# Expert gate/up product: all eight chunks as three fp32r passes, weights split in two halves

## The chip, the cores and the metric

The kernel runs on one core of a Trainium2 chip. The metric is the device time of one execution in microseconds (us). Engines are named as in the profile: PE (TensorE matmuls), PEld (TensorE weight loads), DVE (VectorE), ACT (ScalarE), POOL (GpSimd), SP (SyncE). An engine's name with a q (ACTq) is its instruction queue: register, semaphore and DMA-issuing instructions.

## The reference, cut to what matters

An encoder layer (attention, then a hierarchical mixture of experts) over 3072 tokens. The change touches only the experts. Tokens are sorted by expert into blocks of 128 rows, and each block runs one expert's gated MLP:

```python
D_MODEL, D_EXPERT, N_EXPERTS, MOE_BLOCK = 1024, 256, 32, 128

def run_block(args):
    tok, e = args
    xe = x[tok]                                           # 128 x 1024
    hid = jax.nn.silu(xe @ w_gate[e]) * (xe @ w_up[e])    # 128 x 256
    return hid @ w_down[e]                                # 128 x 1024
```

All of it is float32. A float32 product is made on PE in one of two ways: as one float32 matmul, or split, where each operand is a rounded part (hi, type fp32r) and the rest (lo, fp32r), and three fp32r matmuls hi·hi, hi·lo and lo·hi are summed in PSUM.

## The kernel before

The stages follow one another: projections, attention, output mix, routing, experts (`stage_experts`, from 3508 to 4208 us of the span), combine. In the expert stage there are 64 live blocks here. `over_blocks` runs them in pairs: blocks 0 and 1 written out, then a loop over pairs, whose number is read from a register. Each engine has its own hand-ordered body per block b, and s is b's parity. Nothing but semaphores ties the engines together, so the order within an engine's body is the order in which its work runs.

What one block needs: `x[s]` (gathered by POOL), its transpose in PSUM (`psX`, eight 128x128 transposes, `x_turn`), the gate/up product in `psG` (128 x 512: 256 gate and 256 up columns, over KC = 8 chunks of 128), SiLU (`act_g`) and product (`hid`), the transpose of `hid` (`psH`, `hid_turn`), the down product in `psY` (`down`, always three fp32r passes, 12 matmuls of 128x512), and the copy and store of `y` (`y_out`).

The gate/up product before: chunks 4 to 7 as float32 matmuls straight from `xT` and the loaded weights `w_gu` (L1908), chunks 0 to 3 (HK = 4) as 12 fp32r matmuls (L1913) from `xT_hi`, `xT_lo`, `wg_hi`, `wg_lo`.

The bodies before, for block b:

- PE (`body`): float32 chunks of b, fp32r chunks of b, `hid_turn(b-1)`, `x_turn(b+1)`, `down(b-1)`.
- ACT: `wg_hi` of b (L1792), `xT_hi` of b (L1796), `y_out(b-2)` with its DMA issue (L1811, L1813), `wd_hi` of b (L1806), `hT_hi` of b-1 (L1800), SiLU of b (L1825).
- DVE: copy `xT` (L1837), `xT_lo` (L1839), `wg_lo` (L1845), `wd_lo` (L1857), `hT_lo` of b-1 (L1850), `hid` of b (L1867).
- SP: the expert's weights (3 DMAs of 1 MB) where a block starts a new expert, into a ring of four experts (WS = 4).
- POOL: the gather of `x` one block ahead, released by `x_turn`.

`wg_round`, `wd_round`, `wg_rest` and `wd_rest` begin with `value_load`: the engine's queue reads the ring slot of the block's expert from the SBUF tile `eb` (L1790, L1804, L1843, L1854). `wg_hi` and `wg_lo` have one buffer, `wd_hi` and `wd_lo` two. In the kernel before nothing waits for the release of `wg_hi` by name: `wg_hi` of b stands behind SiLU of b-1 on ACT, which waits for all gate/up matmuls of b-1.

Of the kernel before, what the change touches and what calls it, by code (L numbers as in the profile page):

```python
# [13 lines left out]
P = 128  # L14
# [1652 lines left out]
def stage_experts(nc, t, eb, idx):  # L1667
# [3 lines left out]
    with ExitStack() as ctx:  # L1671
        def sb(name, shape, dt=F32):
            return ctx.enter_context(nc.sbuf_tensor("e_" + name, shape, dt))
# [32 lines left out]
        xT_psum, xT_ready = sem("xT_psum"), sem("xT_ready")  # L1706
# [77 lines left out]
        def _(act):  # L1784
# [3 lines left out]
            def wg_round(b):  # L1788

                w = act.value_load(eb[0:1, bass.ds(b + SLOT_AT, 1)], min_val=0, max_val=WS - 1)  # L1790
                act.wait_ge(w_ready, b + 1)
                nc.scalar.activation(wg_hi[:, :, :], w_gu[:, bass.ds(w * KC, HK), :], ACT.Copy).then_inc(wg_rounded, 1)  # L1792

            def xT_round(b):
                act.wait_ge(xT_psum, b + 3)
                nc.scalar.activation(xT_hi[:, :, :], psX[:, 0, :].rearrange("p (c n) -> p c n", n=P), ACT.Copy).then_inc(xT_rounded, 1)  # L1796

            def hT_round(b):
                act.wait_ge(hT_psum, b + 1)
# [34 lines left out]
        def _(dve):  # L1834
            def xT_out(b):
                dve.wait_ge(xT_psum, b + 3)
                nc.vector.tensor_copy(xT[:, :, :], psX[:, 1, :].rearrange("p (c n) -> p c n", n=P)).then_inc(xT_ready, 1)  # L1837
                dve.wait_ge(xT_rounded, b + 1)
                nc.vector.tensor_tensor(xT_lo[:, :, :], psX[:, 0, :].rearrange("p (c n) -> p c n", n=P),  # L1839
                                        xT_hi[:, :, :].bitcast(F32), ALU.subtract).then_inc(xT_rest_ready, 1)  # L1840

            def wg_rest(b):
                w = dve.value_load(eb[0:1, bass.ds(b + SLOT_AT, 1)], min_val=0, max_val=WS - 1)  # L1843
                dve.wait_ge(wg_rounded, b + 1)
                nc.vector.tensor_tensor(wg_lo[:, :, :], w_gu[:, bass.ds(w * KC, HK), :], wg_hi[:, :, :].bitcast(F32),  # L1845
                                        ALU.subtract).then_inc(wg_ready, 1)
# [13 lines left out]
            def body(b, j, s):  # L1860
# [6 lines left out]
                nc.vector.tensor_tensor(hid[:, s, :], act_g[:, :], psG[:, s, DE:2 * DE], ALU.mult).then_inc(hid_ready, 1)  # L1867

            pairs = over_blocks(dve, body)
            hT_out(2 * pairs - 1)  # L1870

        @block.tensor
        def _(pe):
            def x_turn(b, n, s):
                pe.wait_ge(x_loaded[s], 16 * n + 16)
                pe.wait_ge(xT_ready, b + 1)
# [25 lines left out]
            def body(b, j, s):  # L1902

                w = pe.value_load(eb[0:1, bass.ds(b + SLOT_AT, 1)], min_val=0, max_val=WS - 1)
                pe.wait_ge(w_ready, b + 1)
                pe.wait_ge(xT_ready, b + 2)
                for c in range(HK, KC):
                    nc.tensor.matmul(psG[:, s, :], xT[:, c - HK, :], w_gu[:, bass.ds(w * KC + c, 1), :].rearrange("p o n -> p (o n)"), start=c == HK, stop=False)  # L1908
                pe.wait_ge(xT_rest_ready, b + 1)
                pe.wait_ge(wg_ready, b + 1)  # L1910
                for c in range(HK):
                    for a, ww in ((xT_hi, wg_hi), (xT_hi, wg_lo), (xT_lo, wg_hi)):
                        i = nc.tensor.matmul(psG[:, s, :], a[:, c, :], ww[:, c, :], start=False,  # L1913
                                             stop=c == HK - 1 and ww is wg_hi and a is xT_lo)
                i.then_inc(g_psum, 1)
# [8 lines left out]
            pe.sem_inc(xT_ready, 1)  # L1924
# [222 lines left out]
```

## Time and profile before

| what | value |
|---|---|
| time, median of 3 runs (lowest to highest) | 4388.55 us (4384.7 to 4389.39) |
| span of the profiled execution | 4395.6 us |
| mean granted PE clock | 0.933 |
| PE busy | 3869.2 us (88%) |
| DVE busy | 2832.1 us (64%) |
| ACT busy | 2320.4 us (53%) |
| POOL busy | 415.9 us (9%) |

The span runs from the first to the last instruction of one profiled execution. A row of the timeline reads: start in us from the span's start, duration in us, engine, line, operation, output<-inputs, count, and in brackets the idle time just before it with what ended it; "<-issue" means that the engine's own queue was late. Matmuls are pipelined, so the recorded length of one (0.39 us) is longer than the distance from one start to the next (0.23 us). The granted clock is a share of full speed (2.4 GHz); 0.5 is the other level, 1.2 GHz.

### The profile page before, as it was taken

How to read it: one execution, taken by the hardware profiler on the slowest of the kernel's cores; microseconds unless marked ns; L12 is line 12 of the kernel's file. 1: busy time of each engine (PE TensorE's matmuls, PEld its weight loads, DVE VectorE, ACT ScalarE, POOL GpSimd, SP SyncE). 2: the span in 40 equal slices, each digit the busy share in tenths (PEclk: the TensorE clock that was granted, in tenths of full speed). 3: DMA queues.
4: the chain of work that ended last, by engine and by line, in shares of the span. 5: the costliest groups of instructions: out<-in, count | busy, mean ns of one | idle time of the engine just before them, and what ended most of it. 6: DMA issues, size and time to landing. Idle time of an engine off the chain costs nothing. (4 is left out here: it accounts for less than half of the span.)

```text
span 4395.6 us, 58559 instructions
## 1 busy us (share of the span) xinstructions
PE 3869.2 (88%) x16145; PEld 2606.2 (59%) x16146; DVE 2832.1 (64%) x4533; ACT 2320.4 (53%) x3960; POOL 415.9 (9%) x446
## 2 busy tenths in 40 slices
PE   7999985699999999999999999996999599999920
PEld 3444442366666666666676667664777466666710
DVE  3445454588887888887778677854444556666645
ACT  2222220277777777777666666676333055555521
POOL 0000000011111111111111111100000011111123
PEclk9999996699999999999999999998999699999965
DMA  2343337421122222212211221102333176776658
GB/s 99 105 140 120 125 110 192 155 59 41 24 57 58 59 58 49 46 27 58 57 40 24 57 58 40 24 7 98 134 129 123 39 256 243 254 260 244 240 207 280
DMA packets 295763, 482.81 MB, mean 110 GB/s; under 512 B 117136, under 2 KB 203664, under 8 KB 284750
## 3 DMA queue, kind: packets, MB, share of 16 engines
q1 hardware_dynamic: 207374, 347.24, 26.8%
q10 hardware_dynamic: 71888, 73.54, 4.8%
q0 software_dynamic: 16272, 59.25, 4.0%
q8 instruction: 109, 1.79, 0.2%
q14 instruction: 120, 0.98, 0.1%
HBM read 318.20 MB, written 161.78 MB: 109 GB/s over the span
## 5 line engine op out<-in xcount | busy, mean ns | idle before, releaser
L832 ACT ACTIVATE b_p_hi<-b_psS 128x512 fp32r<-128x512 f32 (+1 forms) x1376 | 821.1, 597 | 620.7 <-PE b_psS L963 579.9
L963 PE MATMUL b_psS<-b_q,b_k 96*128 96x512 f32 (+3 forms) x3440 | 1054.3, 404 | 55.1 <-ACT b_prob L835 31.9
L880 DVE TENSOR_TENSOR b_p_lo<-b_prob,b_p_hi 128x512 fp32r<-128x512 f32 x1152 | 829.0, 721 | 291.0 <-ACT b_prob L835 250.5
L835 ACT ACTIVATE b_prob<-b_psS 128x512 f32<-128x512 f32 (+1 forms) x1376 | 815.3, 593 | 1.1
L963 PEld LDWEIGHTS b_psS<-b_q,b_k 96*128 96x128 f32 (+3 forms) x3440 | 630.1, 186 | 286.5 <-ACT b_prob L835 39.5
L888 DVE TENSOR_REDUCE b_mx_s<-b_psM 128x1 f32<-128x512 f32 x1024 | 691.1, 687 | 80.9 <-PE b_psM L994 67.3
L994 PE MATMUL b_psM<-b_k,b_q 128*128 128x512 f32 (+1 forms) x1280 | 515.3, 424 | 58.1 <-DMA b_v<-V 45.9
L986 PE MATMUL b_psO<-b_p_hi,b_v_hi 128*65 128x512 f32 x1280 | 516.7, 404 | 26.1 <-DVE b_p_lo L880 24.3
L986 PE MATMUL b_psO<-b_p_hi,b_v_lo 128*65 128x512 f32 x1280 | 509.7, 398 | 0.0
L986 PE MATMUL b_psO<-b_p_lo,b_v_hi 128*65 128x512 f32 x1280 | 509.5, 398 | 0.0
L510 PE MATMUL a_psZ<-a_w_in,a_xT 128*128 128x512 f32 (+1 forms) x1200 | 405.9, 498 | 20.0 <-DMA a_w_in<-w_in 10.6
L994 PEld LDWEIGHTS b_psM<-b_k,b_q 128*128 128x128 f32 (+1 forms) x1280 | 251.7, 197 | 161.4 <-DVE b_mx_s L888 49.2
L510 PEld LDWEIGHTS a_psZ<-a_w_in,a_xT 128*128 128x128 f32 x1200 | 207.6, 190 | 219.3 <-issue 195.1
L821 POOL TENSOR_TENSOR b_p_lo<-b_prob,b_p_hi 128x512 fp32r<-128x512 f32 x128 | 167.5, 1309 | 1718.4 <-ACT b_prob L835 1718.4
L986 PEld LDWEIGHTS b_psO<-b_p_lo,b_v_hi 128*65 128x65 f32 x1280 | 175.8, 137 | 125.3 <-issue 5.5
L986 PEld LDWEIGHTS b_psO<-b_p_hi,b_v_hi 128*65 128x65 f32 x1280 | 176.8, 138 | 119.6 <-DVE b_p_lo L880 53.8
L986 PEld LDWEIGHTS b_psO<-b_p_hi,b_v_lo 128*65 128x65 f32 x1280 | 177.6, 139 | 110.5 <-issue 4.2
L1908 PE MATMUL e_psG<-e_w_gu,e_xT 128*128 x512 | 233.2, 598 | 9.4 <-SPq L1755 8.4
L1857 DVE TENSOR_TENSOR e_wd_lo<-e_w_dn,e_wd_hi 128x2048 fp32r<-128x2048 f32 x64 | 146.7, 2293 | 102.9 <-ACT e_wd_hi L1806 102.9
L888 DVE TENSOR_REDUCE b_mx_p<-b_psM 128x1 f32<-128x512 f32 x256 | 173.9, 687 | 30.8 <-PE b_psM L994 27.7
L287 ACT ACTIVATE a_z<-a_psZ,a_rstd 128x1184 f32<-128x1184 f32 x25 | 31.2, 1248 | 292.5 <-PE a_psZ L510 292.5
L1792 ACT ACTIVATE e_wg_hi<-e_w_gu 128x2048 fp32r x64 | 122.9, 1920 | 97.4 <-SPq L1755 75.1
(242 smaller groups left out, 4808.5 us busy)
## 6 DMA issues: line engine op xcount, KB each, us to landing
e_w_gu<-w_gate SPq DMA_DIRECT2D x32, 1024.0 KB
e_w_gu<-w_up SPq DMA_DIRECT2D x32, 1024.0 KB
e_w_dn<-w_down SPq DMA_DIRECT2D x32, 1024.0 KB
Y<-e_y ACTq DMA_DIRECT2D x64, 512.0 KB, 5.3
Y<-b_zeros ACTq DMA_DIRECT2D x4, 4096.0 KB, 27.2
a_x<-xall SPq DMA_DIRECT2D x25, 512.0 KB, 3.8
c_o<-O SPq DMA_DIRECT2D x24, 512.0 KB, 5.0
c_x<-xall SPq DMA_DIRECT2D x24, 512.0 KB, 3.6
```

Of the source, the lines that this page charges most:

```text
L510: i = nc.tensor.matmul(psZ[:, lo:hi], xT[:, c, :], w_in[:, c, lo:hi], start=c == 0, stop=c == KC - 1)
L821: nc.gpsimd.tensor_tensor(p_lo[:, slot, :], prob[0:kn, slot, :], p_hi[0:kn, slot, :].bitcast(F32), ALU.subtract).then_inc(lo_ready_pool, 1)
L832: nc.scalar.activation(p_hi[0:kn, (s * NI + j) % NP, :], psS[0:kn, j % 2, :], ACT.Exp)
L835: nc.scalar.activation(prob[0:kn, (s * NI + j) % NP, :], psS[0:kn, j % 2, :], ACT.Exp).then_inc(p_ready, 1)
L880: nc.vector.tensor_tensor(out, prob[0:kn, slot, :], p_hi[0:kn, slot, :].bitcast(F32), ALU.subtract).then_inc(lo_ready, 1)
L888: nc.vector.tensor_reduce(dst, psM[:, u % 2, :], AX.X, ALU.max).then_inc(m_free, 1)
L963: m = nc.tensor.matmul(psS[0:kn, j % 2, :], kk[s][0:r, k], qq[s][0:r, q], start=n == 0, stop=n == len(passes) - 1)
L986: m = nc.tensor.matmul(psO[0:VC, b % 2, :], vv[s][:, vc, :], pp[:, slot, :], start=first and n == 0, stop=last and n == 2)
L994: nc.tensor.matmul(psM[:, u % 2, :], q0[s][0:r, q * P:q * P + P], k0[s][0:r, kc:kc + 512], start=True, stop=True).then_inc(m_psum, 1)
L1792: nc.scalar.activation(wg_hi[:, :, :], w_gu[:, bass.ds(w * KC, HK), :], ACT.Copy).then_inc(wg_rounded, 1)
L1857: nc.vector.tensor_tensor(wd_lo[:, c, :], w_dn[:, bass.ds(w * HC, HC), :], wd_hi[:, c, :].bitcast(F32), ALU.subtract).then_inc(wd_ready, 1)
L1908: nc.tensor.matmul(psG[:, s, :], xT[:, c - HK, :], w_gu[:, bass.ds(w * KC + c, 1), :].rearrange("p o n -> p (o n)"), start=c == HK, stop=F ...
```

## The change

All eight chunks of gate/up are made as three fp32r passes. `xT` and its copy are gone, `xT_hi` and `xT_lo` have all eight chunks, `wg_hi` and `wg_lo` too, but they are filled in two halves of four chunks, each half in one buffer. ACT rounds a half (`wg_round(b, half)`), DVE makes its rest (`wg_rest(b, half)`), and PE runs 12 matmuls per half. A new semaphore `half_done` tells that the first half's matmuls of a block are done; ACT waits for it before it writes the first half of the next block. The small operations are reordered: `hT_hi`/`hT_lo` of b-2, SiLU and `hid` of b-1, and `wd_hi`/`wd_lo` of b-1 stand now in the body of b, and `y_out(b-2)` is the last of ACT's body. The diff, cut to its core:

```diff
-        xT = sb("xT", [P, KC - HK, P])
-        xT_hi, xT_lo = sb("xT_hi", [P, HK, P], F32R), sb("xT_lo", [P, HK, P], F32R)
-        wg_hi, wg_lo = sb("wg_hi", [P, HK, 2 * DE], F32R), sb("wg_lo", [P, HK, 2 * DE], F32R)
+        xT_hi, xT_lo = sb("xT_hi", [P, KC, P], F32R), sb("xT_lo", [P, KC, P], F32R)
+        wg_hi, wg_lo = sb("wg_hi", [P, KC, 2 * DE], F32R), sb("wg_lo", [P, KC, 2 * DE], F32R)
...
-            def wg_round(b):
+            def wg_round(b, half):
 
                 w = act.value_load(eb[0:1, bass.ds(b + SLOT_AT, 1)], min_val=0, max_val=WS - 1)
                 act.wait_ge(w_ready, b + 1)
-                nc.scalar.activation(wg_hi[:, :, :], w_gu[:, bass.ds(w * KC, HK), :], ACT.Copy).then_inc(wg_rounded, 1)
+                nc.scalar.activation(wg_hi[:, half * HK:half * HK + HK, :], w_gu[:, bass.ds(w * KC + half * HK, HK), :],
+                                     ACT.Copy).then_inc(wg_rounded, 1)
...
             def body(b, j, s):
-                wg_round(b)
+                if at_least(b, 1):
+                    act.wait_ge(half_done, b)
+                wg_round(b, 0)
+                if at_least(b, 2):
+                    hT_round(b - 2)
+                if at_least(b, 1):
+                    silu(b - 1, 1 - s)
                 xT_round(b)
-                if not isinstance(b, int) or b > 1:
-                    y_out(b - 2, j - 1, s)
-                wd_round(b, s)
-                if not isinstance(b, int) or b > 0:
-                    hT_round(b - 1)
-                act.wait_ge(g_psum, b + 1)
-                act.wait_ge(hid_ready, b + 1)
-                nc.scalar.activation(act_g[:, :], psG[:, s, 0:DE], ACT.Silu).then_inc(silu_ready, 1)
+                wg_round(b, 1)
+                if at_least(b, 1):
+                    wd_round(b - 1, 1 - s)
+                if at_least(b, 2):
+                    y_out(b - 2, j - 1, s)
...
+            # DVE
             def body(b, j, s):
-                xT_out(b)
-                wg_rest(b)
-                wd_rest(b, s)
-                if not isinstance(b, int) or b > 0:
-                    hT_out(b - 1)
-                dve.wait_ge(silu_ready, b + 1)
-                nc.vector.tensor_tensor(hid[:, s, :], act_g[:, :], psG[:, s, DE:2 * DE], ALU.mult).then_inc(hid_ready, 1)
+                wg_rest(b, 0)
+                if at_least(b, 2):
+                    hT_out(b - 2)
+                if at_least(b, 1):
+                    hid_out(b - 1, 1 - s)
+                xT_out(b)
+                wg_rest(b, 1)
+                if at_least(b, 1):
+                    wd_rest(b - 1, 1 - s)
...
+            # PE
             def body(b, j, s):
 
-                w = pe.value_load(eb[0:1, bass.ds(b + SLOT_AT, 1)], min_val=0, max_val=WS - 1)
-                pe.wait_ge(w_ready, b + 1)
-                pe.wait_ge(xT_ready, b + 2)
-                for c in range(HK, KC):
-                    nc.tensor.matmul(psG[:, s, :], xT[:, c - HK, :], w_gu[:, bass.ds(w * KC + c, 1), :].rearrange("p o n -> p (o n)"), start=c == HK, stop=False)
-                pe.wait_ge(xT_rest_ready, b + 1)
-                pe.wait_ge(wg_ready, b + 1)
-                for c in range(HK):
-                    for a, ww in ((xT_hi, wg_hi), (xT_hi, wg_lo), (xT_lo, wg_hi)):
-                        i = nc.tensor.matmul(...)
-                i.then_inc(g_psum, 1)
+                pe.wait_ge(xT_rest_ready, b + 2)
+                for half in range(2):
+                    pe.wait_ge(wg_ready, 2 * b + half + 1)
+                    for c in range(half * HK, half * HK + HK):
+                        for a, ww in ((xT_hi, wg_hi), (xT_hi, wg_lo), (xT_lo, wg_hi)):
+                            i = nc.tensor.matmul(psG[:, s, :], a[:, c, :], ww[:, c, :], ...)
+                    i.then_inc(g_psum if half else half_done, 1)
```

The rest of PE's body (`hid_turn(b-1)`, `x_turn(b+1)`, `down(b-1)`) is as before. After the last pair, ACT runs `hT_hi` of the last block but one, SiLU and `wd_hi` of the last block, `y_out`, `hT_hi` of the last block, `y_out`; DVE's end answers to it.

## Rows read from the trace of the kernel before

**Rows 1.** Windows: us, busy us (count) of PE, PEld, DVE, ACT, POOL, clock, DMA.
```profile
3600.00:3700.00 100.00, 99.24 (x405) 69.33 (x404) 64.62 (x56) 56.97 (x58) 10.24 (x18) 1.00 0.70 246
3800.00:3900.00 100.00, 99.15 (x410) 70.25 (x409) 63.89 (x59) 57.77 (x58) 11.26 (x20) 1.00 0.72 256
```

**Rows 2.** Groups by line and form, 3540 to 4190 us: busy us, mean ns | idle before.
```profile
L1908 PE MATMUL e_psG<-e_w_gu,e_xT 128*128 x496 | 222.9, 592 | 0.6 <-SPq L1755 0.6
L1845 DVE TENSOR_TENSOR e_wg_lo<-e_w_gu,e_wg_hi 128x2048 fp32r<-128x2048 f32 x63 | 144.4, 2293 | 11.4 <-issue 11.4
L1792 ACT ACTIVATE e_wg_hi<-e_w_gu 128x2048 fp32r x62 | 119.1, 1921 | 28.2 <-issue 21.9 <-SPq L1755 6.2
...
L1811 ACT ACTIVATE e_y<-e_psY 128x1024 f32<-128x1024 f32 x62 | 63.5, 1023 | 34.4 <-PE e_psY L1897 34.4
...
L1839 DVE TENSOR_TENSOR e_xT_lo<-e_psX,e_xT_hi 128x512 fp32r<-128x512 f32 x62 | 42.9, 692 | 103.2 <-ACT e_xT_hi L1796 103.2
...
L1850 DVE TENSOR_TENSOR e_hT_lo<-e_psH,e_hT_hi 128x256 fp32r<-128x256 f32 x62 | 26.3, 425 | 14.7 <-ACT e_hT_hi L1800 11.3
```

**Rows 3.** Timeline, one block's turn from its gate/up product to the next.
```profile
3859.41 3.59 PE L1908 MATMUL e_psG<-e_w_gu,e_xT 128*128 x8
...
3863.07 0.40 PE L1913 MATMUL e_psG<-e_wg_lo,e_xT_hi 128*128 128x512 f32 x1
...
3865.35 0.40 PE L1913 MATMUL e_psG<-e_wg_hi,e_xT_lo 128*128 128x512 f32 x1
...
3865.82 1.06 PE L1879 MATMUL e_psX<-e_ident,e_x 128*128 128x128 f32 x8
3866.02 0.38 ACT L1800 ACTIVATE e_hT_hi<-e_psH 128x256 fp32r<-128x256 f32 x1 [2.15 <-PE e_psH L1886]
...
3866.44 0.42 DVE L1850 TENSOR_TENSOR e_hT_lo<-e_psH,e_hT_hi 128x256 fp32r<-128x256 f32 x1
3866.78 0.41 DVE L1867 TENSOR_TENSOR e_hid<-e_act_g,e_psG 128x256 f32<-128x256 f32 x1
...
3866.96 0.47 PE L1897 MATMUL e_psY<-e_wd_hi,e_hT_hi 128*128 128x512 f32 x1
...
3869.80 2.74 PE L1908 MATMUL e_psG<-e_w_gu,e_xT 128*128 x6
```

**Rows 4.** Timeline, ACT and DVE around a store and a weight split.
```profile
3860.91 0.37 ACTq L1813 DMA_DIRECT2D Y<-e_y  x1
...
3861.95 1.92 ACT L1806 ACTIVATE e_wd_hi<-e_w_dn 128x2048 fp32r x1 [1.22 <-issue]
...
3864.02 2.29 DVE L1857 TENSOR_TENSOR e_wd_lo<-e_w_dn,e_wd_hi 128x2048 fp32r<-128x2048 f32 x1 [1.55 <-ACT e_wd_hi L1806]
```

**Rows 5.** Line 1790, the slot's read on ACT's queue: ns min/median/max.
```profile
L1790 ACTq TENSOR_LOAD <-eb x64: 274/280/288, 3509.1 to 4182.5; - x64
```

**Rows 6.** Timeline, the starts of blocks 2 and 63 on PE.
```profile
3547.60 3.59 PE L1908 MATMUL e_psG<-e_w_gu,e_xT 128*128 x8
...
4186.14 3.59 PE L1908 MATMUL e_psG<-e_w_gu,e_xT 128*128 x8
```

**Rows 7.** Timeline, the start of the stage: blocks 0 and 1.
```profile
3524.81 1.91 ACT L1792 ACTIVATE e_wg_hi<-e_w_gu 128x2048 fp32r x1 [68.90 <-SPq L1755]
3524.86 6.58 PE L1908 MATMUL e_psG<-e_w_gu,e_xT 128*128 x8 [7.78 <-SPq L1755]
...
3534.23 0.38 ACT L1825 ACTIVATE e_act_g<-e_psG 128x256 f32<-128x256 f32 x1 [3.92 <-PE e_psG L1913]
...
3540.53 0.47 PE L1913 MATMUL e_psG<-e_wg_hi,e_xT_hi 128*128 128x512 f32 x1 [0.75 <-DVE e_wg_lo L1845]
3540.84 0.39 PE L1913 MATMUL e_psG<-e_wg_lo,e_xT_hi 128*128 128x512 f32 x1
```

**Rows 8.** Timeline, the longest stall of PE in the stage and what follows.
```profile
4021.59 0.47 PE L1913 MATMUL e_psG<-e_wg_hi,e_xT_hi 128*128 128x512 f32 x1 [1.92 <-DVE e_wg_lo L1845]
...
4022.49 0.63 PE L1913 MATMUL e_psG<-e_wg_hi,e_xT_hi 128*128 128x512 f32 x1
4022.91 0.63 PE L1913 MATMUL e_psG<-e_wg_lo,e_xT_hi 128*128 128x512 f32 x1
```

**Rows 9.** Windows of 5 us around that stall, columns as in Rows 1.
```profile
4020.00:4025.00 5.00, 3.41 (x9) 2.72 (x10) 3.74 (x2) 1.92 (x1) 0.00 (x0) 0.72 0.83 284
```

More of the change, by code:

```diff
@@ L1705, in stage_experts @@
         cur_ready = sem("cur_ready")
-        xT_psum, xT_ready = sem("xT_psum"), sem("xT_ready")
+        xT_psum, half_done = sem("xT_psum"), sem("half_done")
         g_psum, silu_ready, hid_ready = sem("g_psum"), sem("silu_ready"), sem("hid_ready")
@@ L1734, in is_last, with at_least @@
             return isinstance(b, int) and b == BLOCKS - 1
+        def at_least(b, n):
+            return not isinstance(b, int) or b >= n
         @block.sync
@@ L1806, in wd_round, with silu @@
                 nc.scalar.activation(wd_hi[:, s * HC:(s + 1) * HC, :], w_dn[:, bass.ds(w * HC, HC), :], ACT.Copy).then_inc(wd_rounded, 1)
+            def silu(b, s):
+                act.wait_ge(g_psum, b + 1)
+                act.wait_ge(hid_ready, b + 1)
+                nc.scalar.activation(act_g[:, :], psG[:, s, 0:DE], ACT.Silu).then_inc(silu_ready, 1)
             def y_out(b, j, s):
@@ L1858, in wd_rest, with hid_out, body @@
                                         ALU.subtract).then_inc(wd_ready, 1)
[L1860 to L1865 removed]
+            def hid_out(b, s):
                 dve.wait_ge(silu_ready, b + 1)
                 nc.vector.tensor_tensor(hid[:, s, :], act_g[:, :], psG[:, s, DE:2 * DE], ALU.mult).then_inc(hid_ready, 1)
+            def body(b, j, s):
+                wg_rest(b, 0)
[7 more added lines that the diff above has]
+                    wd_rest(b - 1, 1 - s)
             pairs = over_blocks(dve, body)
+            hT_out(2 * pairs - 2)
+            hid_out(2 * pairs - 1, 1)
+            wd_rest(2 * pairs - 1, 1)
             hT_out(2 * pairs - 1)
@@ L1902, in body @@
             def body(b, j, s):
-                w = pe.value_load(eb[0:1, bass.ds(b + SLOT_AT, 1)], min_val=0, max_val=WS - 1)
-                pe.wait_ge(w_ready, b + 1)
-                pe.wait_ge(xT_ready, b + 2)
-                for c in range(HK, KC):
-                    nc.tensor.matmul(psG[:, s, :], xT[:, c - HK, :], w_gu[:, bass.ds(w * KC + c, 1), :].rearrange("p o n -> p (o n)"), start=c == HK, stop=False)
-                pe.wait_ge(xT_rest_ready, b + 1)
-                pe.wait_ge(wg_ready, b + 1)
-                for c in range(HK):
-                    for a, ww in ((xT_hi, wg_hi), (xT_hi, wg_lo), (xT_lo, wg_hi)):
-                        i = nc.tensor.matmul(psG[:, s, :], a[:, c, :], ww[:, c, :], start=False,
-                                             stop=c == HK - 1 and ww is wg_hi and a is xT_lo)
-                i.then_inc(g_psum, 1)
+                pe.wait_ge(xT_rest_ready, b + 2)
[3 more added lines that the diff above has]
+                        for a, ww in ((xT_hi, wg_hi), (xT_hi, wg_lo), (xT_lo, wg_hi)):
+                            i = nc.tensor.matmul(psG[:, s, :], a[:, c, :], ww[:, c, :], start=c == 0 and ww is wg_hi and a is xT_hi,
+                                                 stop=c == KC - 1 and a is xT_lo)
+                    i.then_inc(g_psum if half else half_done, 1)
                 some_before = not isinstance(b, int) or b > 0
```

26 lines of the change are left out of this document (15 added, 11 removed).

## The prediction, made before the changed kernel was run

> **What bounds the kernel now.** I read the windows first. Inside the expert stage PE is busy 99 us of every 100 at full clock, ACT 57 and DVE 64 [rows 1]. So PE sets the pace, and the groups by line show that its matmuls wait for almost nothing: the float32 group has 0.6 us of idle time in 650 us, while DVE and ACT wait in every block [rows 2]. The timeline of one turn then gives the price list. A block starts at 3859.41 and the next at 3869.80, so a turn costs 10.39 us [rows 3]. Over blocks 2 to 63 the mean is (4186.14 - 3547.60) / 61 = 10.47 us [rows 6]; the 0.08 us more come from a few late weights and stalls, 5 us in all. The reader should see that PE has no slack in a turn, and that ACT and DVE have over 3.5 us each. The question is whether the new order keeps PE fed.
>
> **PE's own work.** The gate/up product now takes from 3859.41 to 3865.35 + 0.23, 6.17 us [rows 3]. The fp32r matmuls follow each other at (3865.35 - 3863.07) / 10 = 0.228 us. The change makes 24 of them: 5.47 us, 0.70 less. The two and eight transposes stay at 1.2 us, `down` stays at 3869.80 - 3866.96 = 2.84 us, and 0.15 us lie between [rows 3]. If PE stayed the bound, a turn would be 9.69 us. That is the gain on offer: 0.70 x 64 = 45 us.
>
> **Work that ACT and DVE get.** ACT: a second `wg_hi` half (1.92), `xT_hi` over 1024 instead of 512 columns; the nearest row is the copy of `y`, also 1024 columns from PSUM, 1.02 us [rows 2], against 0.58 before. DVE: a second `wg_lo` half (2.29), the copy `xT` gone (-0.69), `xT_lo` over 1024 columns. 256 columns took 0.425 and 512 took 0.692 [rows 2], so 1024 take 0.692 + 2 x 0.267 = 1.23 us; the upper bound is twice 0.692, 1.38. Sums per turn: ACT 3 x 1.92 + 2 x 1.02 + 2 x 0.38 = 8.6 us, plus the DMA issue and the register read behind the copy of `y`, which is the 1.2 us before `wd_hi` [rows 4], 9.8. DVE 3 x 2.29 + 1.23 + 0.42 + 0.41 = 8.9 us. Both fit under 10.39, though with little slack. By sums alone the change would pay. But both engines run their lists in order, and the lists now form a loop with PE.
>
> **The wait that is added, and who stands behind it.** ACT may write `wg_hi`'s first half of block b only when `half_done` says that PE has finished the first 12 matmuls of b-1. Behind that `wg_hi` on ACT, and behind its `wg_lo` on DVE, stand `hT_lo` of b-2, `hid` of b-1 and `xT_lo` of b. `hT_lo` of b-2 releases `down(b-2)` on PE, and `down(b-2)` stands in PE's list before the first half of b. So there is a closed chain: first half of b-1 → `wg_hi` → `wg_lo` → `hT_lo` → `down` → first half of b. Before, the 2.3 us of `wg_lo` and the 1.9 us of `wg_hi` stood after `hT_lo`, under `down` and the float32 matmuls.
>
> Its length, step by step from the end H of the last first-half matmul:
>
> 1. Semaphore to ACT 0.04 (`hT_hi` ends 3866.40, `hT_lo` starts 3866.44, rows 3), then the register read, which stands after the wait in ACT's queue. From the end of the DMA issue at 3861.28 to `wd_hi` at 3861.95 it is 0.67 us [rows 4]. The read alone is 0.28 [rows 5], the rest address work. Bounds 0.28 and 1.2 (the whole gap of rows 4); I take 0.67, the same sequence. Together 0.71.
> 2. `wg_hi`, 1.92 [rows 2].
> 3. ACT to DVE with address work: `wd_hi` ends 3863.87, `wd_lo` starts 3864.02, 0.15 [rows 4].
> 4. `wg_lo`, 2.29 [rows 2].
> 5. `hT_lo`, 0.42, of which 0.07 overlap with what runs before it (as `hid` at 3866.78 starts 0.08 before `hT_lo` ends): 0.35 [rows 3].
> 6. To the first `down` matmul: 3866.96 - 3866.86 = 0.10 [rows 3].
> 7. `down`, 2.84 to the next group's start.
> 8. First half of b: 11 x 0.228 + 0.40 until its last one has ended, 2.91.
>
> The sum is 0.71 + 1.92 + 0.15 + 2.29 + 0.35 + 0.10 + 2.84 + 2.91 = 11.27 us. That is over PE's own 9.69, and over today's 10.39.
>
> What runs beside it, counted from H: PE starts the second half at -0.17 and is through it at 2.56, through `hid_turn` and `x_turn` at 3.8. `down` then waits for `hT_lo`, which starts at 5.0 and not at 3.4, where `hT_hi` ends: `down` starts at 5.52, a stall of about 1.7 us in every turn. `xT_hi` runs 3.9 to 4.9, `hid` 5.4 to 5.8, `xT_lo` 5.7 to 6.9, and PE wants it at 8.4: 1.5 us early, so its bound of 1.38 changes nothing. `wg_hi`'s second half is done at 6.7, `wg_lo`'s at 9.2, and PE wants it at 11.1. `wd_hi` ends at 8.6, `wd_lo` at 11.5, wanted at 16.8. `y_out` copies from 8.6, after `down` has ended, and its DMA issue is through at 10.2, before ACT's next wait ends at 11.27; with the loop's branches (some 0.3 us) still 0.7 early. Stores, gathers (POOL, still released by `x_turn`) and SP's weight loads (still released by `down`) keep their places and move with the turn. If that cover went, ACT's late 0.7 us is the next price. The register reads of PE's body go, but they were hidden behind queued matmuls: 0.
>
> **Start and end.** Block 0 on PE starts today with the weights, at 3524.86, and its product is there at 3534.2 [rows 7]. Now it waits for `wg_hi`, `wg_lo` and, behind that on DVE, `xT_lo`: 3524.8 + 1.9 + 0.2 + 2.3 + 1.2 = 3530.4. PE has stood idle and is at its 1.2 GHz level, where matmuls came every 0.43 us [rows 8]: 12 of them 5.1 us, then 2.7 at full clock, product at 3538.3, 4 us later than now. Two more turns of 0.9 us each: block 2 starts 6 us late. At the end the last `wd_lo` comes 4.7 us after the last product and `down` of the block before takes at least that long, so 0; bounds -0.7 (PE's shorter product) and +3.
>
> **The sum.** 61 turns x (11.27 - 10.47) = +48.8 us, start +6, end 0, less some 2 us because late weights have more time: +52.8. In the profiled execution 4395.6 becomes 4448; the runs' median lies 7 us below the span, so 4388.6 + 52.8 = 4441 us. With the register read at 0.28 it is 4417, at 1.2 it is 4474.
>
> **Rivals.**
>
> *The stall drops PE's clock as well.* PE stood 1.92 us before the matmul at 4021.59, and from about 4022.1 the granted clock is at its 1.2 GHz level: 0.72 in that window of 5 us [rows 9], matmuls 0.43 apart instead of 0.228 for eight of them, 1.6 us lost [rows 8]. A stall of 0.75 us at 3540.5 was followed by 0.31 and then full speed [rows 7]. My stall of 1.7 us lies near the longer one, and it decides somewhere between them. The lost time falls on `down` and the first half, which are links of the chain, so it counts in full: in every second turn +49 us, 4490; in every turn +98, 4540. For it: the stall comes 60 times. Against it: it is shorter than the one case, and the transposes before it keep PE at work. The Trainium skill, "TensorE: Matmul & The Clock Gate", section "A second HAM failure mode: psum-queue depth-cycling", tells of frequent short idle times between groups of matmuls that let the clock swing between its two levels. By that rule the clock would fall in every turn; the trace agrees for 1.92 us and not for 0.75.
>
> *PE stays the bound, the kernel is faster.* One turn is 9.69 us: 61 x -0.78 + 6 = -42 us, 4347. It holds if `hT_lo` is not kept back, which needs `wg_lo`'s first half to end before 3.4 us after H. The two splits alone are 4.2 us, so it needs the release to come 1.7 us earlier than I read it (a wait that is met by an earlier block). Against it stands the count: `half_done` rises by one per block and is waited for at b. For it only that I may have misread the counts.
>
> *The chain is shorter than its sum.* If the register read ran ahead of the wait and the hand-overs overlapped, 10.4 to 10.9 us per turn: no change to +32 us, 4389 to 4420. The read stands behind the wait in program order, so I give it little.
>
> *The change doesn't do what it says.* PE's records will show 24 fp32r matmuls or not; nothing in the diff leaves one float32.
>
> **How the numbers follow.** Forecast (4420 to 4460): 0.64. Clock falls too: 0.20, of which 0.12 up to 4495 and 0.08 above. Shorter chain: 0.08, of which 0.02 within 0.2%. PE-bound and faster: 0.08. 0.2% (9 us) is about what a measurement of this kernel can tell from no change. The range 4412 to 4495 takes in the bounds of the register read, most of the shorter chain and the milder clock case: 0.64 + 0.12 + 0.04 = 0.8. Faster 0.08, same 0.02, slower 0.90.
>
> **What would show it.** In the profile after: starts of first halves 11.2 to 11.3 us apart; before each `down` an idle time of PE of 1.6 to 1.8 us that ends with DVE's `hT_lo`; `hT_lo` starting right as `wg_lo` ends; `wg_hi`'s first half starting 0.7 us after the last first-half matmul; ACT idle before it; PE busy about 86% of the stage. The granted clock stays 1.00 in the stage's windows by the forecast, and below by the first rival. Wrong it would be if `down` starts right after `x_turn`, or if PE waits elsewhere (for `xT_lo`, or the second half).

## The result, and the profile after

The changed kernel runs 4526.8 us (median of 4 runs, 4519.0 to 4533.5), the kernel before 4389.0 beside it. The ratio is 1.031, 95% interval 1.030 to 1.033. The forecast was 4441 with a range of 4412 to 4495: the direction was right, the size (+52 forecast, +138 measured) was not. The profiled execution took 4519.0 us with a span of 4517.2; the span of before was 4395.6.

Windows of the changed kernel, columns as in rows 1, and one window of 5 us:

```profile
3600.00:3700.00 100.00, 84.41 (x369) 69.29 (x368) 67.92 (x48) 65.81 (x56) 18.74 (x16) 0.91 0.60 209
3800.00:3900.00 100.00, 84.40 (x368) 69.47 (x368) 67.49 (x49) 65.60 (x56) 18.92 (x16) 0.91 0.61 210
...
3915.00:3920.00 5.00, 4.47 (x13) 3.55 (x14) 5.00 (x6) 3.05 (x2) 1.09 (x2) 0.66 1.05 403
```

PE is busy 84 of 100 us, where it was 99 [rows 1], and no other engine has become full: DVE 68, ACT 66. That is the picture of a chain through several engines, not of a new bound. And the granted clock is 0.91 where it was 1.00.

Groups by line and form, 3540 to 4190 us, columns as in rows 2:

```profile
L1859 DVE TENSOR_TENSOR e_wg_lo<-e_w_gu,e_wg_hi 128x2048 fp32r<-128x2048 f32 x105 | 240.2, 2288 | 210.5 <-ACT e_wg_hi L1794 210.5
L1794 ACT ACTIVATE e_wg_hi<-e_w_gu 128x2048 fp32r x105 | 201.0, 1915 | 145.7 <-issue 60.0 <-PE e_psG L1932 56.0 <-SPq L1757 29.7
...
L1920 PE MATMUL e_psY<-e_wd_hi,e_hT_hi 128*128 128x512 f32 x204 | 100.4, 492 | 99.7 <-issue 99.7
...
L1852 DVE TENSOR_TENSOR e_xT_lo<-e_psX,e_xT_hi 128x1024 fp32r<-128x1024 f32 x52 | 63.3, 1218 | 0.0
...
L1864 DVE TENSOR_TENSOR e_hT_lo<-e_psH,e_hT_hi 128x256 fp32r<-128x256 f32 x51 | 21.3, 417 | 0.0
```

Before, PE waited for almost nothing [rows 2]. Now it is idle 99.7 us before the first matmul of `down` (204 / 4 = 51 blocks, 1.95 us each). The profile names "issue" as the releaser there: it has no engine to blame, so the timeline must. `hT_lo` has no idle time before it any more (0.0 against 14.7): it starts out of a full DVE queue, right behind `wg_lo`. DVE itself waits 210 us, all of it for `wg_hi`. A `down` matmul is recorded with 492 ns in mean. The same group before had 413 ns, and 5.3 us of idle time in all:

```profile
L1897 PE MATMUL e_psY<-e_wd_hi,e_hT_hi 128*128 128x512 f32 x248 | 102.4, 413 | 5.3
```

Timeline of one turn (start, duration, engine, line, operation, idle time before):

```profile
3906.62 0.39 PE L1932 MATMUL e_psG<-e_wg_hi,e_xT_hi 128*128 128x512 f32 x1
...
3908.12 0.37 ACTq L1821 DMA_DIRECT2D Y<-e_y  x1
...
3909.14 0.39 PE L1932 MATMUL e_psG<-e_wg_hi,e_xT_lo 128*128 128x512 f32 x1
...
3910.73 1.92 ACT L1794 ACTIVATE e_wg_hi<-e_w_gu 128x2048 fp32r x1 [2.78 <-issue]
...
3912.33 1.06 PE L1902 MATMUL e_psX<-e_ident,e_x 128*128 128x128 f32 x8
3912.56 0.36 ACT L1803 ACTIVATE e_hT_hi<-e_psH 128x256 fp32r<-128x256 f32 x1
3912.80 2.29 DVE L1859 TENSOR_TENSOR e_wg_lo<-e_w_gu,e_wg_hi 128x2048 fp32r<-128x2048 f32 x1 [4.84 <-ACT e_wg_hi L1794]
...
3915.01 0.42 DVE L1864 TENSOR_TENSOR e_hT_lo<-e_psH,e_hT_hi 128x256 fp32r<-128x256 f32 x1
...
3915.53 0.48 PE L1920 MATMUL e_psY<-e_wd_hi,e_hT_hi 128*128 128x512 f32 x1 [2.14 <-issue]
...
3916.24 0.63 PE L1920 MATMUL e_psY<-e_wd_hi,e_hT_lo 128*128 128x512 f32 x1
3916.67 0.63 PE L1920 MATMUL e_psY<-e_wd_hi,e_hT_hi 128*128 128x512 f32 x1
...
3919.95 0.39 PE L1932 MATMUL e_psG<-e_wg_hi,e_xT_hi 128*128 128x512 f32 x1
```

The chain can be read off link by link: the last first-half matmul ends at 3909.53, `wg_hi` starts 1.20 later, `wg_lo` behind it, `hT_lo` at the moment `wg_lo` is done, `down` 0.10 after `hT_lo`. `hT_hi` was ready at 3912.92 and lay there for 2.1 us. Then comes what the forecast had only as a rival: matmuls of 0.63 us, 0.43 apart, which is the 1.2 GHz level of the clock, and a `down` of 3919.95 - 3915.53 = 4.42 us instead of 2.84.

Counted over blocks 2 to 62, a turn is 12.43 us in mean (before: 10.47). In 26 of 60 turns `down` keeps its 2.84 us and the turn is mostly 11.35 to 11.65 (11.56 in mean, one of 12.11); in 34 it mostly takes 4.2 to 4.4 and the turn is 12.7 to 13.3 (13.10 in mean).

**Where the 121.6 us of the spans went.** The 60 turns are 60 x 1.96 = 118 us longer. Block 2 starts 12.2 us later, of which 4.3 us lie ahead of the first `wg_hi` (3529.09 against 3524.81, rows 7), where the change has no part, and 7.9 us after it. The end of the stage adds 2. The stages behind it, which are untouched, ran 10 us shorter in this execution. 118 + 12 + 2 - 10 = 122. The median of the changed kernel's runs lies 10 us above its span, before it lay 7 us below; the runs spread over 14 us, and no trace shows those of them that were not profiled.

### The profile page after: what moved, and what is told of

Read it like the earlier page. It is cut to its first block and busy times, and to the rows that moved or that the text cites. A ratio compares the mean times of both kernels' runs of the same rounds, so it can differ in the third digit from the quotient of the medians.

```text
span 4517.2 us, 59357 instructions
## 1 busy us (share of the span) xinstructions
PE 3882.6 (86%) x16401; PEld 2698.2 (60%) x16401; DVE 2949.1 (65%) x4533; ACT 2465.2 (55%) x4024; POOL 490.1 (11%) x446
## 5 line engine op out<-in xcount | busy, mean ns | idle before, releaser
L1859 DVE TENSOR_TENSOR e_wg_lo<-e_w_gu,e_wg_hi 128x2048 fp32r<-128x2048 f32 x128 | 292.8, 2287 | 269.5 <-ACT e_wg_hi L1794 269.5
L1794 ACT ACTIVATE e_wg_hi<-e_w_gu 128x2048 fp32r x128 | 245.0, 1914 | 242.8 <-SPq L1757 108.5
L1920 PE MATMUL e_psY<-e_wd_hi,e_hT_hi 128*128 128x512 f32 x256 | 126.3, 493 | 121.8 <-issue 121.7
L1932 PE MATMUL e_psG<-e_wg_hi,e_xT_hi 128*128 128x512 f32 x512 | 203.2, 397 | 17.7 <-DVE e_xT_lo L1852 17.7
L1771 POOL CAST e_cur<-idx 128x1 uint32 x65 | 86.2, 1327 | 1090.3 <-PE e_psX L1902 579.0
```

What stands on the lines that cost most here:

```text
L1794: nc.scalar.activation(wg_hi[:, half * HK:half * HK + HK, :], w_gu[:, bass.ds(w * KC + half * HK, HK), :], ACT.Copy).then_inc(wg_rounded, 1)
L1859: nc.vector.tensor_tensor(wg_lo[:, c, :], w_gu[:, bass.ds(w * KC + half * HK, HK), :], wg_hi[:, c, :].bitcast(F32), ALU.subtract).then_inc ...
```

## The experiments

Experiments 1 to 5 and 8 are a few lines away from the changed kernel; the others move more, as said there. "Ratio" is to the kernel before, run beside it. The stall is PE's idle time before `down`; a slow `down` is one of over 3.2 us. Times are medians, but turns and stalls come from the one profiled execution of each kernel, which need not be a typical one. All eleven kernels came out slower than expected, ten by 15 to 60 us and one by 148: the sums counted the link that was moved, and not what becomes late next.

**1. The register read ahead of the wait.** On ACT, the slot of the weights is read from memory into a register before the wait for `half_done`, not behind it.

```
-                if at_least(b, 1):
-                    act.wait_ge(half_done, b)
                 wg_round(b, 0)
...
                 w = act.value_load(eb[0:1, bass.ds(b + SLOT_AT, 1)], min_val=0, max_val=WS - 1)
+                if half == 0 and at_least(b, 1):
+                    act.wait_ge(half_done, b)
                 act.wait_ge(w_ready, b + 1)
```

> Edit: in ACT's list the slot read for the first half of wg_hi stands before the wait for half_done instead of behind it; nothing else moves. Theory (one closed chain from the first-half matmuls over wg_hi, wg_lo, hT_lo and down back to them, with the register read as a link, and a clock that falls when PE's stall is about 2 us long): the gap from the last first-half matmul to wg_hi shrinks from 1.0 to about 0.15 us, the stall before down from 2.0 to 1.2 us, the clock stays at full speed, a turn takes 10.7 us instead of 12.4 on average, and the time is about 4389 + 5 + 61 x 0.23 = 4408 us. Rival A (the clock falls whatever the stall's length): a turn of 10.7 plus the same 0.85 us of slow down matmuls, 4460 us. Rival B (the read ran ahead and is not in the chain): no change, 4527 us.

Measured: 4467.8 us, ratio 1.018 (1.016 to 1.020), 59 us less than the change. Turns alternate: 10.73 us in one parity, as worked out, and 11.46 in the other, some of those 13. In the first, `wg_hi` starts 0.21 us after the last first-half matmul; in the second it is 0.87 to 0.97. There the read stands at the head of the loop, where ACT first has 0.36 us of branches and then a read of 0.7 to 0.8 us, so it comes too late to lie under the wait. The read is a link of the chain, and the stall goes with it (1.15 to 1.2 us in the short turns); `down` is slow in 9 of 60 turns instead of 34, all but one of them in the longer parity. The expected 4408 was missed by 60 us, because half of the turns kept the read in the chain. The time lies near rival A's, but its condition doesn't hold: none of the 29 stalls of 0.6 to 1.3 us was followed by a slow `down`. The profiled execution is the fastest of five (4445.4), so the trace shows the better case.

**2. The register read twice.** The opposite: one more read behind the wait.

```
                     act.wait_ge(half_done, b)
+                    act.value_load(eb[0:1, bass.ds(b + SLOT_AT, 1)], ...)
                 wg_round(b, 0)
```

> Edit: one more slot read (result unused) behind the wait for half_done on ACT. Theory (read in the chain, clock falls with the stall): 0.5 to 1.0 us more per turn without a fall, 12.1 us, the stall before down 2.6 us or more and so a fall of the clock in nearly every turn, 1.6 us each, 13.7 us, time 4389 + 6 + 61 x 3.2 = 4590 us. Rival A (clock independent of the stall): 61 x 0.6 = 37 us over the changed kernel, 4564 us. Rival B (read hidden): 4527 us.

Measured: 4608.4 us, ratio 1.048 (1.045 to 1.052), turns of 13.73 us in mean, stall 2.63, `down` slow in 57 of 60 turns. A window (columns as in rows 1):

```profile
3800.00:3900.00 100.00, 78.82 (x329) 64.58 (x329) 63.67 (x47) 60.48 (x54) 23.37 (x16) 0.87 0.56 194
```

The added read at line 1826 and the old one (ns, lowest/median/highest, as in rows 5):

```profile
L1826 ACTq TENSOR_LOAD <-eb x63: 276/491/877, 3536.7 to 4386.7; - x63
...
L1792 ACTq TENSOR_LOAD <-eb x128: 272/278/1257, 3507.7 to 4390.5; - x128
```

One read, which makes the turns without a clock fall 0.7 us longer, costs 82 us: 60 x 0.7 = 42 by the chain, and 23 more slow `down`s x 1.5 = 35 by the clock. The first read behind the wait takes 0.49 in median, the second right behind it 0.28 in median, but over 0.3 in 24 of 63.

**3. Work for PE in the stall.** Eight float32 matmuls of 128x128 on the identity, into a PSUM bank that nothing else uses, stand ahead of `down`. The chain is not touched; PE only has more to do.

```
                     x_turn(b + 1, j + s, 1 - s)
                 if some_before:
+                    for _ in range(8):
+                        nc.tensor.matmul(psF[:, 0:P], ident[:, :], ident[:, :], start=True, stop=True)
                     down(b - 1, 1 - s)
```

> Edit: between x_turn and down PE makes eight float32 matmuls of 128x128 of the identity into a PSUM bank of their own, 0.21 us each, 1.7 us in all, from block 1 on. They depend on nothing and nothing waits for them, so the closed chain's length is the same and only PE's stall is filled. Theory (the stall costs the clock): down takes 2.84 us in every turn, turns are 11.5 us (now 11.4 to 11.6 without a fall of the clock and 13.1 with one), the granted clock is 1.00 in the stage, and the time is 4389 + 6 + 61 x 1.05 = 4459 us. Rival A (the clock falls for another reason, such as the denser fp32r matmuls): down still takes 4.4 us in half the turns, 4527 us or more. Rival B (PE's own work is the bound): 1.7 us more per turn, over 4600 us.

Measured: 4477.5 us, ratio 1.020 (1.016 to 1.023). A window:

```profile
3800.00:3900.00 100.00, 98.46 (x543) 84.70 (x542) 72.63 (x54) 72.07 (x62) 21.15 (x18) 1.00 0.61 214
```

The timeline around one stall, with the filling matmuls of line 1943 (each float32 matmul leaves two records, so eight are x16):

```profile
3907.83 1.95 PE L1943 MATMUL e_psF<-e_ident 128*128 128x128 f32 x16
...
3909.86 0.47 PE L1921 MATMUL e_psY<-e_wd_hi,e_hT_hi 128*128 128x512 f32 x1
```

With more work and nothing else changed the kernel is 49 us faster. `down` takes 2.84 us in 59 of 60 turns, the clock is 1.00, and the turns are 11.3 to 11.6 us but for four: the chain alone, as in the change's turns without a clock fall (11.56 in mean). One turn is 17.16 us for late weights, where the change's longest is 13.33, so the clock's share is rather some 5 us more than the 49. This separates the two causes: the stall's own time stays (4477 against 4389), the clock's share is the rest. PE is busy 98 of 100 us here, and it is still 2% slower than before: a busy share says nothing of what the work is good for.

**4. `hT_lo` ahead of `wg_lo`, on DVE only.**

```
             def body(b, j, s):
-                wg_rest(b, 0)
                 if at_least(b, 2):
                     hT_out(b - 2)
+                wg_rest(b, 0)
                 if at_least(b, 1):
                     hid_out(b - 1, 1 - s)
```

> Edit: one line moved in DVE's body, hT_lo of b-2 before the first half's wg_lo of b. Nothing else. Theory: down no longer waits for wg_lo, its stall shrinks from 2.0 to 0.2 us, but the first half of the next block now waits for xT_lo, which stands behind the later wg_lo: 1.4 us there. A turn without a fall of the clock is 11.15 us instead of 11.5; the stall of 1.4 us is under the 1.7 us from which falls were seen, so few falls: 4389 + 6 + 61 x 0.69 = 4437 us. Rival A (the chain over hT_lo was not the bound): 4527 us. Rival B (it was the only one): 9.7 to 10.4 us per turn, 4350 to 4395 us.

Measured: 4462.9 us, ratio 1.016 (1.013 to 1.019), 64 us less by one line's place. PE's groups from 3560 to 4190 us:

```profile
L1932 PE MATMUL e_psG<-e_wg_hi,e_xT_hi 128*128 128x512 f32 x440 | 177.3, 403 | 73.1 <-DVE e_xT_lo L1852 73.1
...
L1920 PE MATMUL e_psY<-e_wd_hi,e_hT_hi 128*128 128x512 f32 x222 | 91.7, 413 | 13.4 <-issue 10.5
```

The idle time before `down` is gone (13.4 us in all) and turns up before the first half of the next block, where PE waits for `xT_lo` (73.1). So `wg_lo` ahead of `hT_lo` was what kept `down` back; taking it away shows the next in the same queue, at 11.44 us a turn. Split over two places (0.23 us before `down` and 1.33 before the first half, in mean) the idle time costs no clock: it is granted in full in all 60 turns.

**5. Most of the first half's `wg_lo` left out.** This kernel leaves out part of the work: `wg_lo` of the first half has one column of each chunk, and PE's second pass of that half reads `wg_hi` again. PE's work and all waits stay; DVE is 2.1 us shorter in the chain (0.17 instead of 2.29).

```
                 c = slice(half * HK, half * HK + HK)
+                n = 2 * DE if half else 1
-                nc.vector.tensor_tensor(wg_lo[:, c, :], ...
+                nc.vector.tensor_tensor(wg_lo[:, c, 0:n], ...
```

> This kernel leaves out part of the computation: DVE makes only one column of the first half's wg_lo, and PE's second pass of that half reads wg_hi instead (the same count and size of matmuls). Everything else is the changed kernel. Theory: the chain loses 2.0 us of its 11.5 and is shorter than PE's own 9.7 us and ACT's list of about 9.9 us with its reads and its store; no stall before down, full clock, a turn of 9.8 to 10.0 us, 4389 + 3 - 61 x 0.57 = 4357 us. Rival A (24 fp32r matmuls cost PE as much as what they replace): 10.4 us, 4389 us. Rival B (the wait is on something else than wg_lo): the stall stays, over 4460 us.

Measured: 4388.7 us, ratio 0.998 (0.996 to 0.999): all of the 138 us are gone, though the turns alternate between 9.67 and 10.58 us. Two turns of 16.47 and 18.67 us, in which ACT waits for late weights, take 15 us of the gain. The windows have PE at 94.5 and the clock at 1.00. The short turns are PE's own time, for which the prediction had 9.69. The long ones start at the loop's head, as in experiment 1.

**6. The hidden state's transposes between the halves.** On PE `hid_turn` moves between the two halves, `hT_hi` and `hT_lo` to the head of ACT's and DVE's bodies, `hid` behind `xT_lo`, and the register read ahead of the wait. `wg_lo` then has the second half and `down` for cover.

```
                     i.then_inc(g_psum if half else half_done, 1)
+                    if half == 0 and at_least(b, 1):
+                        hid_turn(b - 1, 1 - s)
                 some_before = not isinstance(b, int) or b > 0
-                if some_before:
-                    hid_turn(b - 1, 1 - s)
```

> Edit: hid_turn(b-1) goes between PE's two halves of block b, hT_hi and hT_lo of b-2 stand first in ACT's and DVE's bodies, hid of b-1 stands behind xT_lo of b on DVE, and the slot read stands before the wait for half_done. The same work is done. Theory: hT_lo no longer stands behind the first-half wg_lo, the chain is open, and PE's own work is the bound: a turn of 9.7 to 9.9 us, no stall before down, full clock, time 4389 + 5 - 61 x 0.65 = 4354 us (4343 to 4370), faster than the kernel before. Rival A (DVE's list is the next bound, since 8.9 us of work are in it): 10.2 us or more, 4378 us. Rival B (the three fp32r passes save PE nothing): 10.4 us, 4389 us or more.

Measured: 4399.1 us, ratio 1.001 (1.000 to 1.002). No stall before `down`, clock 1.00, turns alternating 9.93 and 10.55. PE's and ACT's groups:

```profile
L1932 PE MATMUL e_psG<-e_wg_hi,e_xT_hi 128*128 128x512 f32 x484 | 201.2, 416 | 43.1 <-DVE e_xT_lo L1852 42.9
...
L1796 ACT ACTIVATE e_wg_hi<-e_w_gu 128x2048 fp32r x122 | 233.9, 1917 | 55.4 <-issue 27.7 <-SPq L1757 27.7
```

It is 128 us better than the change and equal to the kernel before within what the runs can tell; 4354 was expected. What is late next is `xT_lo`, behind the read (0.6 to 1.0 us) on ACT.

**7. The same with the register read once for two blocks,** at the head of the loop; the second block's slot is read ahead of `wd_hi` and kept.

```
             def body(b, j, s):
+                w = slot(b) if s == 0 else kept["next"]
                 if at_least(b, 2):
                     hT_round(b - 2)
...
+                if s == 0:
+                    kept["next"] = slot(b + 1)
```

> Edit: the kernel of e4 with fewer slot reads on ACT: the slot of a block is read once and kept for wg_hi's second half and for wd_hi, the odd block's slot is read in the even block's body under a running ACTIVATE, so the only read that ACT waits for is at the loop's head. Theory (in e4 the register read behind hT_hi, 0.7 us, made wg_hi late and through wg_lo and xT_lo kept PE 0.9 us from the next block): the odd blocks' first wg_hi starts right behind hT_hi, PE's stall before the first half goes in these turns, 9.7 us, and stays at up to 0.7 us in the others, 10.2 us; 9.95 on average, 4389 + 5 - 61 x 0.52 = 4362 us, faster than before. Rival (DVE's list of 8.9 us with its own reads is the bound): turns stay at 10.4 us as in e4, 4399 us.

Measured: 4389.3 us, ratio 0.999 (0.997 to 1.001). One turn of each pair is now 9.48 us. The other is 10.99: at the head of the loop ACT comes 1.6 to 2.1 us late to `hT_hi`.

```profile
3847.39 0.38 ACT L1808 ACTIVATE e_hT_hi<-e_psH 128x256 fp32r<-128x256 f32 x1 [2.11 <-issue]
```

**8. The copy and store of `y` ahead of `wd_hi`,** in the changed kernel. I meant it to bring the store away from the register read.

```
+                if at_least(b, 2):
+                    y_out(b - 2, j - 1, s)
                 if at_least(b, 1):
                     wd_round(b - 1, 1 - s)
-                if at_least(b, 2):
-                    y_out(b - 2, j - 1, s)
```

> The changed kernel with one move: y_out (copy of y and issue of the Y store) stands ahead of wd_hi in ACT's body, no longer behind it. The issue of the store then lies about 2 us or more ahead of the register read that follows the wait for half_done; nothing else in the chain is touched, and wd_hi still ends long before it is wanted. Theory (the read is slow because it follows closely behind the store's DMA issue): the gap from the last first-half matmul to wg_hi falls from 1.01 to 0.70-0.75 us, the stall before down from 1.95 to 1.65-1.7, turns of 11.25-11.35 where the clock stays; since stalls of 1.7-1.9 us were followed by the lower clock in 3 of 17 and 8 of 25 turns, down is slow in 0 to 20 of 60 turns. Time 4440 to 4470, best guess 4455. Rival (the read is slow because it is the first instruction behind a wait, whatever stood before): gap 1.0, stall 1.95, time as the changed kernel's 4527 within 10 us.

Measured: 4602.6 us, ratio 1.048 (1.046 to 1.051). A miss by 150 us. ACT's timeline shows why:

```profile
3904.45 1.03 ACT L1819 ACTIVATE e_y<-e_psY 128x1024 f32<-128x1024 f32 x1 [4.29 <-PE e_psY L1920]
3905.65 0.37 ACTq L1821 DMA_DIRECT2D Y<-e_y  x1
3906.79 1.92 ACT L1809 ACTIVATE e_wd_hi<-e_w_dn 128x2048 fp32r x1 [1.31 <-issue]
3908.62 1.90 ACT L1794 ACTIVATE e_wg_hi<-e_w_gu 128x2048 fp32r x1
```

The copy of `y` waits for `down`, and everything behind that wait waits with it. `wd_hi` (1.92) had run while PE did `down`; now it starts 1.3 us after the copy, and `wg_hi` can start only when it is through: from the end of `down` the way over ACT is 4.3 us, longer than the first half's 2.9. I had read "`wd_hi` ends long before it is wanted" from PE's side and had not asked what comes behind it on ACT. It is the fault that the change itself makes, repeated by me: a step with a late wait set ahead of one that had cover. The stall is 2.69 us in mean, `down` slow in 45 turns of 60. So it can't tell what the read after a store costs, for which it was meant.

**9. The kernel of experiment 7 with `y` stored ahead of `wd_hi`; 10. and with `hT_hi` ahead of the read as well.** There `down` has ended long before ACT comes to the copy, so the copy's wait is free. The first has the diff of experiment 8, the second this one more:

```
-                w = slot(b) if s == 0 else kept["next"]
                 if at_least(b, 2):
                     hT_round(b - 2)
+                w = slot(b) if s == 0 else kept["next"]
```

> The kernel with the hidden turn between the halves and one slot read at the loop's head (which ran 4389, turns alternating 9.48 and 11.0), and y_out ahead of wd_hi. Theory (the long turn comes from ACT's branch and slow slot read behind the store at the loop's head, which make hT_hi, wg_hi and xT_lo late): the read behind the loop's branch goes back to 0.3 us, ACT's idle time before hT_hi falls from 1.6-2.1 to about 1.0 us, long turns 10.4, short ones 9.5: mean 9.95, about 25 us below that kernel, ratio to the kernel before 0.993 (some 4360). Rival (ACT is full anyway and wd_hi coming later makes wd_lo late for down): long turns stay 11.0 and a stall before down that ends with wd_lo appears; time 4385 to 4400.

> The one before, and at the loop's head hT_hi stands ahead of the slot read, so that only the branch and not the read holds hT_hi back. Theory: hT_hi 0.3-0.5 us earlier, the read falls behind it ahead of wg_hi; xT_lo 0.3 us earlier at most. Long turns 10.1 to 10.4, mean 9.8 to 9.9, ratio to the kernel before 0.990 to 0.993 (4345 to 4360). Rival (what is late at the loop's head is wg_hi and not hT_hi, and the read is in its way either place): same as the one without this move, within 5 us.

Measured: 4384.6 us, ratio 0.998 (0.996 to 1.000), and 4386.1 us, ratio 0.999 (0.998 to 1.001). The median long turn fell from 10.99 to 10.30 us, as expected; the mean of all turns fell from 10.43 to 10.24, since some short turns grew. In the profiled executions the spans differ by 19 us (4372.4 and 4353.0), in the medians by 5: the profiled execution of experiment 9 is the fastest of its twelve (4354.9 to 4394.4), and its trace doesn't show what makes the others longer. The second move brought nothing. ACT's and PE's groups of the first of the two:

```profile
L1799 ACT ACTIVATE e_wg_hi<-e_w_gu 128x2048 fp32r x120 | 229.8, 1915 | 30.8 <-SPq L1757 30.3
L1939 PE MATMUL e_psG<-e_wg_hi,e_xT_hi 128*128 128x512 f32 x485 | 200.5, 413 | 34.2 <-DVE e_xT_lo L1859 34.0
```

ACT now waits for SP's signal that the weights are there, 7.4 of the 30 us in one turn. One expert's weights land 12.8 us after the issue of their last transfer in median, and the issue waits for a `down` that frees the slot.

**11. The gate/up weights signalled apart from `w_down`,** each in three transfers, in the kernel of experiment 9.

```
-                                 t["w_down"][...]).then_inc(w_loaded, 16)
+                                     t["w_down"][...]).then_inc(d_loaded, 16)
...
                 sp.sem_inc(w_ready, 1)
+                with sp.If(new > 0):
+                    sp.wait_ge(d_loaded, target)
+                sp.sem_inc(d_ready, 1)
...
             def wd_round(b, s, w):
-                act.wait_ge(w_ready, b + 1)
+                act.wait_ge(d_ready, b + 1)
```

> The kernel with y_out ahead of wd_hi and one slot read per pair (which ran 4385, span 4353, turns alternating 9.48 and 10.0 to 11.3, its first wg_hi 20 times held by SP's signal for the weights), with the expert's weights signalled in two parts: the gate/up weights as soon as they have landed (three transfers), w_down by a semaphore of its own (three transfers), which only wd_hi waits for. In that kernel gate/up landed 11.0 us and w_down 12.8 us after their issue, in median, while the loop of the first half of a block wants them about 9.5 + 2.9 = 12.4 us after the slot comes free. Theory (the long turns of that kernel are late weights, not ACT's list): no wait of wg_hi for SP but at one or two blocks, long turns 9.5 to 10.0, mean 9.7 over all but the late one: some 25 to 35 us below that kernel, 4345 to 4360, ratio to the kernel before 0.989 to 0.993. Rival (the long turns come from ACT's branch and register read or from late gathers): ratio 0.997 to 1.000 as before, with the waits of PE for xT_lo unchanged.

Measured: 4398.9 us, ratio 1.001 (0.999 to 1.002). My theory fell. ACT's group has the same wait:

```profile
L1808 ACT ACTIVATE e_wg_hi<-e_w_gu 128x2048 fp32r x121 | 231.7, 1915 | 37.8 <-SPq L1761 37.8
```

ACT waits for SP nearly as often as before (18 times instead of 20) and longer: most turns are 9.5 to 10.1 us, but 14 of 60 are over 11, where it was 6. So it is not `w_down`'s place in the signal. Whether the slots, the order of the loads on SP or the transfers' rate (DMA share 0.74 in experiment 9's windows, 0.61 in the change's) holds them up stays open.

## Why the prediction was off

Two steps failed: the sum put the price of the clock at nothing, where it was 51 us, and step 1 of the chain was 0.30 us too short, 18 us in all.

**What held.** The chain is as the prediction numbered it, and experiments 1, 2, 4 and 5 each changed one link and moved the time. By its steps: `wg_hi` 1.92, handover 0.15, `wg_lo` 2.29, `hT_lo` 0.35, 0.10 to `down`, first half 2.9 all came as read. The new forms were sized well: `xT_lo` 1.22 (forecast 1.23), `xT_hi` 1.02. PE is busy 84% of the stage (forecast 86). Turns without a clock fall, 11.56 in mean, stand 0.3 above the 11.27.

**Step 1 of the chain was too short.** The gap from the last first-half matmul to `wg_hi` was put at 0.71 and measured 1.01 in mean (0.82 to 1.21). In each of the 60 turns it is the read plus 0.55 us. The forecast had 0.28 for the read [rows 5] and 0.43 for the rest [rows 4]. So 0.12 us of the miss are the wait and the address work, and 0.18 are the read itself, for which the changed kernel shows

```profile
L1792 ACTq TENSOR_LOAD <-eb x128: 273/282/661, 3511.8 to 4312.4; - x128
```

Half of these, the reads of the first half, stand behind the wait and take 0.46 us in mean (0.28 to 0.66). The change had put the store of `y` at the end of ACT's body, a microsecond ahead of them. The prediction saw that move, counted its 1.2 us as free, and did not ask whether the read behind it keeps its price; that the store is what slows it is not shown (see the last section). 60 x 0.30 = 18 us. The bound of 1.2 us that it gave covers this.

**The clock was the rival with a chance of 0.20, and it came true.** `down` was slow in 34 of 60 turns, 1.5 us each, 0.85 us per turn over all, 51 us. Experiment 3 takes just this away and gives 49 us back. The prediction had the mechanism and its size (1.6 us, rows 8), and its condition (somewhere between a stall of 0.75 and one of 1.92 us). Two things made it set the chance too low. It took 1.7 us as "shorter than the one case", although the range of its own step 1 carried the stall over 2. And it let the two terms stand apart, though they are one: the same 0.3 us that lengthens the chain lengthens the stall, and so weighs on the clock. Even at the forecast's 1.7 us the clock wouldn't have been free: of the stalls of 1.7 to 1.9 us in the change and in experiment 1, 11 of 42 were followed by the lower clock. The Trainium skill, "TensorE: Matmul & The Clock Gate", section "A second HAM failure mode: psum-queue depth-cycling", had it that frequent short idle times let the clock swing between its levels; the trace agrees in more than half of the turns.

**The start.** +7.9 us against +6; block 0's first 13 matmuls came 0.43 apart, as forecast, and block 1 met a stall of 2.77 us and the lower clock again, which was not counted.

Sum: 60 x 0.80 (the chain as forecast) + 18 (step 1) + 51 (the clock) = 117, and 118 was measured. With the start and the untouched stages that accounts for the span. The forecast also took the runs' median as 7 us below the span, and it lay 10 above: these 16 us stay open.

**Why the offered gain never came.** PE's pure time of 9.5 to 9.7 us per turn is real (experiments 5, 7 and 9 show such turns). To reach it the work between the halves had to be reordered on three engines, and then late weights and the loop's head on ACT took the gain. One late load shows in experiments 1, 3, 5 to 7 and 9 to 11 alike: a turn of 15.5 to 18.8 us at block 46, in which ACT waits 5.4 to 8.7 us for SP. Before, the same place cost less. The two rows, before and in experiment 9:

```profile
4015.86 1.91 ACT L1792 ACTIVATE e_wg_hi<-e_w_gu 128x2048 fp32r x1 [3.76 <-SPq L1755]
...
4005.40 1.91 ACT L1799 ACTIVATE e_wg_hi<-e_w_gu 128x2048 fp32r x1 [7.39 <-SPq L1757]
```

The best version measured, experiment 9, stands at 0.998 of the kernel before (0.996 to 1.000), which is hardly a gain, and 3% below the change.

## What to carry to other kernels

Where an in-order engine gets a long step with a late release, write down all that stands behind it in that queue and ask who waits for each: what is moved behind it loses its cover, however much idle time the engine has by sums. When a chain through several engines leaves PE idle in every turn, take the length of the stall and the clock together: a longer link can cost twice its own length (experiment 2: 82 us for 42), and filling the stall with harmless matmuls tells the two apart in one run. A price read from one place in a queue (a register read of 0.28 us) holds for that place.

## What the runs showed of the hardware

**Register reads behind a store's issue.** Over all the traces, reads on ACT's queue that start within 0.3 us of the end of the issue of the `Y` store, or over 2 us behind it, take 0.28 us, with six exceptions. Those that start in between take 0.49 in median in the change, 0.73 in experiment 1, and 0.31 to 0.85 over the other kernels, 1.67 at most; SP's reads, on another queue, show it too (0.83 in median in the change, from 0.3 to 0.7 us behind the store). Before, none of ACT's reads fell into that time [rows 5]. It doesn't need a wait just ahead: the slow reads of experiment 1 have none. Nor is it sure to happen: in experiment 11 the median there is 0.31. This is a correlation over positions; no run had the store taken away.

**A tiny copy on POOL beside DVE.** The copy of one index column takes 0.185 us in mean before, and 1.39 in the change:

```profile
L1771 POOL CAST e_cur<-idx 128x1 uint32 x53 | 73.5, 1387 | 496.9 <-PE e_psX L1902 496.9
```

It ends when the `wg_lo` that DVE has begun ends (3900.37 + 1.44 against 3899.47 + 2.29). It had slack here.

**Stalls and the clock.** Of PE's stalls before `down` in the change, 3 of 17 between 1.7 and 1.9 us were followed by the lower clock, 28 of 38 between 1.9 and 2.1, and 3 of 5 above. With the read doubled it was 52 of 55 between 2.3 and 3.0 us. With the read first, 0 of 29 between 0.6 and 1.3, and 8 of 25 between 1.7 and 1.9. It isn't the length alone: in experiment 8 none of 15 stalls of 2.1 to 2.3 us had it, every fourth turn.
